# RWKV-7 recurrence of a two-layer decoder step: inverse norms as a power on GpSimd, and another place for the key operations

## What is computed

```python
heads = lambda z: z.reshape(b, t, h, n)               # 16 heads of 64
kk = heads(k * k_k)
kk = kk / jnp.maximum(jnp.linalg.norm(kk, axis=-1, keepdims=True), 1e-12)
k = k * (1 + (a - 1) * k_a)
decay = jnp.exp(-jnp.exp(heads(w)))
# per token: S = S*d - (S kk) (kk*a)^T + v k^T ;  y = S r
mean = jnp.mean(y, axis=-1, keepdims=True)
var = jnp.mean(jnp.square(y - mean), axis=-1, keepdims=True)
y = ((y - mean) * lax.rsqrt(var + RW_GN_EPS)).reshape(b, t, d) * lnx_g + lnx_b
```

## Time and profile before

| what | value |
|---|---|
| median of 3 runs | 3940.99 us (3935.37 to 3941.91) |
| the profiled execution's own time | 3936.94 us |
| its span, first to last instruction | 3935.2 us |
| busy: PE, DVE, ACT, POOL | 93%, 58%, 21%, 19% |
| recurrence, 407 to 1066 us: busy PE, DVE, ACT, POOL | 560.75, 471.37, 252.55, 40.73 us of 659 |
| one pair in the middle, 599 to 675.8 us: the same | 67.32, 59.19, 32.25, 5.22 us of 76.8 |

### The profile page before, as it was taken

One profiled execution on the slowest core, in us unless ns is written; L12 is line 12 of the kernel. 1 busy time (PEld: TensorE's weight loads), 2 busy tenths in 40 slices (PEclk: granted clock), 3 DMA queues, 4 the chain that ended last, 5 costly groups with the idle time before them and its releaser, 6 DMA issues. The chain is left out here.

```text
span 3935.2 us, 73104 instructions
## 1 busy us (share of the span) xinstructions
PE 3673.9 (93%) x31536; PEld 2834.7 (72%) x31536; DVE 2272.5 (58%) x3422; ACT 820.7 (21%) x1836; POOL 742.0 (19%) x504
## 2 busy tenths in 40 slices
PE   7999788888899999999999999999967999999997
PEld 4888566666667888878776777777644788887886
DVE  8442677777456566672646455656546655567253
ACT  6110344433121110110111222222223100101000
POOL 1221000000022222213431100101002222221343
PEclk9999899999999999999999999999989999999999
DMA  2222111011211111122221111111482111112232
GB/s 82 74 81 90 56 36 45 29 36 29 106 39 47 45 45 35 44 75 89 101 79 66 58 40 47 40 47 40 151 307 103 47 45 45 45 43 74 81 113 73
DMA packets 119159, 268.30 MB, mean 68 GB/s; under 512 B 38072, under 2 KB 59960, under 8 KB 116408
## 3 DMA queue, kind: packets, MB, share of 16 engines
q1 hardware_dynamic: 118840, 263.63, 19.4%
HBM read 214.64 MB, written 48.95 MB: 67 GB/s over the span
## 5 line engine op out<-in xcount | busy, mean ns | idle before, releaser
L403 PE MATMUL ps<-sb_h,sb_w 128*128 128x272 f32 x1672 | 408.1, 392 | 1.4 <-ACT sb_tmp L563 1.4
L403 PEld LDWEIGHTS ps<-sb_h,sb_w 128*128 128x128 f32 x1672 | 317.5, 190 | 67.6 <-issue 2.3
L403 PE MATMUL ps<-sb_x,sb_w 128*128 128x272 f32 x1216 | 291.1, 392 | 0.0
L403 PEld LDWEIGHTS ps<-sb_x,sb_w 128*128 128x128 f32 x1216 | 231.0, 190 | 47.6
L460 PE MATMUL ps<-sb_big,sb_w 128*128 128x272 f32 x1056 | 250.9, 396 | 2.5 <-issue 1.3
L460 PEld LDWEIGHTS ps<-sb_big,sb_w 128*128 128x128 f32 x1056 | 202.3, 192 | 46.4 <-issue 4.3
L766 DVE SCALAR_TENSOR_TENSOR sb_big<-sb_tmp,sb_big 128x1024 f32<-128x1024 f32 (+1 forms) x176 | 203.4, 1155 | 13.2
L1454 PE MATMUL ps<-sb_x,sb_w 128*128 128x272 f32 x768 | 183.8, 392 | 0.0
L373 PE MATMUL ps<-sb_h,sb_w 128*128 128x384 f32 (+1 forms) x576 | 177.1, 469 | 3.9 <-DVE sb_tmp L741 2.1
L2693 PE MATMUL ps<-sb_h,sb_w 128*128 128x384 f32 (+1 forms) x528 | 171.8, 468 | 0.0
L1454 PEld LDWEIGHTS ps<-sb_x,sb_w 128*128 128x128 f32 x768 | 145.9, 190 | 30.1
(11 more groups left out here) (413 smaller groups left out, 6972.1 us busy)
## 6 DMA issues: line engine op xcount, KB each, us to landing
sb_w<-wup SPq DMA_DIRECT2D x88, 512.0 KB, 4.5
sb_w<-wdown SPq DMA_DIRECT2D x48, 704.0 KB, 4.2
sb_w<-wqkv SPq DMA_DIRECT2D x33, 512.0 KB, 3.6
sb_w<-wrkv SPq DMA_DIRECT2D x24, 512.0 KB, 5.5
sb_tmp<-wdown SPq DMA_DIRECT2D x16, 704.0 KB, 4.1
sb_x<-kT SPq DMA_DIRECT2D x10, 1024.0 KB, 12.2
rkv_scratch<-sb_big SPq DMA_DIRECT2D x18, 544.0 KB, 6.5
sb_big<-vc SPq DMA_DIRECT2D x9, 1024.0 KB, 11.7
```

The costliest lines, as they stand in the source:

```text
L403: mm = pe.matmul(m.ps[:, 2 * HOME[f][p] + e, 0:PIECE], w, rhs[:, k, e * PIECE:(e + 1) * PIECE], start=(k == 0 and p not in ("P2", "P3")), ...
```

## The change

The root on ACT and the reciprocal on DVE of both norms go. For the key norm DVE takes the sums out of PSUM with a maximum (`square_sums`, behind `t0`) and POOL raises them to the power -0.5; for the norm of y ACT writes scaled sums plus epsilon (`variances`) and POOL raises those. The exponent is a column of -0.5 read again and again. PE waits for POOL, by a new semaphore. `keys` moves from ahead of level 1 to behind level 2. ACT's program holds 26 table loads instead of 39: those of L1723 and L1758 are gone, and one comes in front of the first root of `tail` (L513), whose table the recurrence used to leave behind.

```diff
-    ACTS = numbered([(0, "squares"), (0, "roots"), (0, "powers"), (0, "inverses")],
-                    [(1, "squares"), (0, "queries"), (1, "roots"), (1, "powers"), (1, "inverses"), (-1, "deviations"),
-                     (-1, "deviation_roots"), (0, "U")], [(LAST, "deviations"), (LAST, "deviation_roots")])
+    ACTS = numbered([(0, "squares"), (0, "powers"), (0, "inverses")],
+                    [(1, "squares"), (0, "queries"), (1, "powers"), (1, "inverses"), (-1, "deviations"),
+                     (-1, "variances"), (0, "U")], [(LAST, "deviations"), (LAST, "variances")])
+    NORMS = numbered([(0, "key")], [(1, "key"), (-1, "y")], [(LAST, "y")])
...
         @block.gpsimd
         def _(pool):
             pool.memset(qm, 0.0).then_inc(zeroed, 1)
+            power = m.small[:, 22:23].broadcast_to([P, LANE])
+            pool.memset(m.small[:, 22:23], -0.5)
+            pool.drain()
+
+            def key_norm(j):
+                pool.wait_ge(prep_d, prepared(j, "sums"))
+                pool.tensor_tensor(rootk, rootk, power, ALU.pow).then_inc(normed_by, 1)
+
+            def y_norm(i):
+                pool.wait_ge(acts, ACTS[i, "variances"])
+                pool.tensor_tensor(rootv, rootv, power, ALU.pow).then_inc(normed_by, 1)
+
+            key_norm(0)
             pool.wait_ge(consts, 8 * 16)
             for i in range(PAIRS):
                 for half, (c0, c1) in enumerate(((0, 8), (8, NCH))):
                     wait_taken(pool, i, "at", half)
                     pool.tensor_tensor(AMc[:, c0:c1, :], ATc[:, c0:c1, :], bc(lm[:, 0, :], c1 - c0), ALU.mult).then_inc(am, 1)
+                if i < LAST:
+                    key_norm(i + 1)
+                if i:
+                    y_norm(i - 1)
                 pool.wait_ge(acts, ACTS[i, "U"])
...
+            y_norm(LAST)
...
-            def roots(j):
+            def powers(j):
                 act.wait_ge(small_ps, SUMS[j, "keys"])
-                act.activation(rootk, m.ps[:, 6, 0:LANE], ACT.Sqrt).then_inc(acts, 1)
-
-            def powers(j):
                 act.wait_ge(prep_d, prepared(j, "diff"))
                 act.activation(EP, LS, ACT.Exp, scale=-DEC).then_inc(acts, 1)
...
-            def deviation_roots(i):
+            def variances(i):
                 act.wait_ge(small_ps, SUMS[i, "vars"])
-                act.activation(rootv, m.ps[:, 6, 0:LANE], ACT.Sqrt, bias=m.eps[:, 1:2], scale=1.0 / HD).then_inc(acts, 1)
+                act.activation(rootv, m.ps[:, 6, 0:LANE], ACT.Identity, bias=m.eps[:, 1:2], scale=1.0 / HD).then_inc(acts, 1)
...
-                if ahead:
-                    roots(ahead)
                 turned_out(i, "z0", Yc)
                 if ahead:
                     powers(ahead)
...
-            def inverse_norms(j):
-                dve.wait_ge(acts, ACTS[j, "roots"])
-                dve.tensor_scalar(rootk, rootk, 1e-12, None, ALU.max)
-                dve.drain()
-                dve.reciprocal(rootk, rootk).then_inc(prep_d, 1)
+            def square_sums(j):
+                dve.wait_ge(small_ps, SUMS[j, "keys"])
+                dve.tensor_scalar(rootk, m.ps[:, 6, 0:LANE], 1e-24, None, ALU.max).then_inc(prep_d, 1)
...
-            def inverse_deviations(i):
-                dve.wait_ge(acts, ACTS[i, "deviation_roots"])
-                dve.reciprocal(rootv, rootv).then_inc(gn_d, 1)
...
-            inverse_norms(0)
+            square_sums(0)
...
                 from_one(i, "t0", Xc)
                 if ahead:
-                    keys(ahead)
+                    square_sums(ahead)
                 for l in range(1, 6):
                     level(i, l)
                     if l == 1 and i:
                         center(i - 1)
                     if l == 2 and ahead:
-                        inverse_norms(ahead)
-                    if l == 4 and i:
-                        inverse_deviations(i - 1)
+                        keys(ahead)
                     if l < 5:
                         update(i, f"x{l}", Xc)
...
             def key_norms(j):
-                pe.wait_ge(prep_d, prepared(j, "inv"))
+                pe.wait_ge(normed_by, NORMS[j, "key"])
                 spread(j, "kn", rootk)
...
                 if i + 2 < PAIRS:
-                    pe.wait_ge(acts, ACTS[i + 2, "roots"])
+                    pe.wait_ge(prep_d, prepared(i + 2, "sums"))
...
             def var_norms(i):
-                pe.wait_ge(gn_d, i + 1)
+                pe.wait_ge(normed_by, NORMS[i, "y"])
                 spread(i, "vn", rootv)
```

More of the change, by code:

```diff
@@ L1530, in rwkv_core @@
         full, outd, outa, am = (sem(n) for n in ("psum_full", "dve_out", "act_out", "level_mask"))
-        prep_d, gn_d, acts, small_ps = (sem(n) for n in ("prep_dve", "norm_dve", "act_done", "small_psum"))
+        prep_d, acts, small_ps, normed_by = (sem(n) for n in ("prep_dve", "act_done", "small_psum", "norms"))
         sampw, stp, std, sst, masked, done = (sem(n) for n in ("sample_w", "state_psum", "state", "sample_state", "batch_masked", "pair_done"))
@@ L1572, in rwkv_core @@
         heads = (slice(0, 64), slice(64, 128))
-        EVENTS = ("q0", "diff", "inv", "rkr", "ready")
+        EVENTS = ("q0", "diff", "sums", "rkr", "ready")
         FLAT = ((0, 2 * 384), (2 * 384, T))
@@ L1578, in prepared @@
             if i == 0:
-                return ("q0", "diff", "inv", "keyed", "rkr", "ready").index(event) + 1
+                return ("q0", "diff", "sums", "keyed", "rkr", "ready").index(event) + 1
             return 5 * i + EVENTS.index(event) + 2
@@ L1763, in _ @@
             squares(0)
-            roots(0)
             powers(0)
@@ L1790, in _ @@
                 if i:
-                    deviation_roots(i - 1)
+                    variances(i - 1)
                 turned_out(i, "z3", Yc, PC)
@@ L1806, in _ @@
             deviations(LAST)
-            deviation_roots(LAST)
+            variances(LAST)
         @block.vector
@@ L2059, in _ @@
             center(LAST)
-            inverse_deviations(LAST)
             normed(LAST)
@@ L2308, in _ @@
                 if i:
-                    pe.wait_ge(acts, ACTS[i - 1, "deviation_roots"])
+                    pe.wait_ge(acts, ACTS[i - 1, "variances"])
                 else:
-                    pe.wait_ge(acts, ACTS[1, "roots"])
+                    pe.wait_ge(prep_d, prepared(1, "sums"))
                 pe.wait_ge(ld_s, 16 * (i + 1))
```

## The result

| | before | changed |
|---|---|---|
| median of 4 runs each | 3938.55 us | 4458.4 us (4450.22 to 4464.87) |
| ratio | | 1.1307, 95% interval 1.1291 to 1.1323 |
| span of the profiled execution | 3935.2 us | 4460.4 us |
| mean granted clock of PE | 0.982 | 0.922 |
| recurrence, DVE's first row to PE's first L348 | 658.8 us | 1174.4 us |

The forecast was 3935.9 us, with 3972 as the end of its range. The change costs 520 us between the medians and 525.2 between the two profiled executions; of these 525.2 the recurrence holds 515.6.

What follows compares the result with a forecast made beforehand. No engine is full in the recurrence; PE and DVE wait for each other, DVE late at level 1. 8.4 + 1.3 + 0.8 gained plus 3.8 - 2P at the ends gave 3935.9 us at P = 4.6, range 3927 to 3972.

Steps and rivals of the forecast that it cites:

- The power on POOL: Time P of one power for a norm on POOL: taken as 4.6 us, upper end 13.9.
- Where P shows: Hidden in the middle of a pair up to P = 8.5 us; uncovered at the recurrence's start and end.
- P - 1.7 us lost: Start of the recurrence, where nothing covers the power: 2.9 us lost with P = 4.6.
- P - 2.1: End of the recurrence, PE's spread waiting for the power: 2.5 us lost with P = 4.6.
- 14.3 - 2P: Whole sum: 10.5 us gained in the pairs plus 3.8 - 2P for both ends; 5.1 us less at P = 4.6.
- level 1: Keys moved away, so DVE takes `t1` sooner and PE's wait goes: 1.2 us a pair, 8.4 us for seven.
- level 2: Keys take the place of maximum and reciprocal there: 0.18 us a pair gained, 1.3 us for seven.
- level 4: The y norm's reciprocal on DVE goes, nearly hidden before: 0.12 us a pair, 0.8 us for seven.
- a cheap power: Rival: P near POOL's plain product, 11.5 us gained, 3929.5 us; chance 0.34.
- A dear power: Rival: P above 8.5, PE waits at the y spread in seven pairs and both ends; 3958 us at 9.3; chance 0.22.
- The port held throughout: Rival: a shared port holds DVE's key operations to the end of POOL's power; 4028 us at P = 13.9; chance 0.03.
- Gain taken back: Rival: PE's 1.18 us wait reappears at `x1` or the means, level 1 yields nothing; 3944.3 us; chance 0.06.

Runs made afterwards that it cites:

- Experiment 1: The changed kernel with both powers on POOL replaced by a plain product with a constant, norms not computed: 3932.48 us, ratio 0.9974.
- experiment 6: The kernel before with keys behind level 2 and POOL's power for the key norm only, y by root and reciprocal: 4086.65 us.
- experiment 2: The kernel before with keys behind level 2, the key norm's maximum and reciprocal behind level 3, no POOL work: 3933.16 us, ratio 0.9978.
- experiment 3: The kernel before with both norms on ACT as exponential of a logarithm, keys behind level 2: 3932.57 us, ratio 0.998; repeated 3932.45 us.
- experiment 7: The kernel of experiment 3 with the keys behind level 3 instead of level 2: 3926.69 us, ratio 0.995; repeated 3923.99 us, ratio 0.9954.

## Why the prediction was wrong

**The power on POOL** is the step that failed: the term P of the sum, "0.75 x 6.2 = 4.6 us, which I take", and its bound, "13.9, the upper end". Measured 43.70, 58 times the 0.75 us product it was scaled from (68 times the 0.639 us product in its own place). The scale came from DVE's reciprocal on this tile, another function on another engine, and nothing in the trace of before tied the two; the bound from above rested on how many such steps a power might be made of, which is no measurement either. The Trainium skill's page GPSIMD Engine Reference, section "Side-by-side cycle accounting", with its some 12 cycles for an element in the dearest case, had given an estimated 2.7 us. By the 1.2 GHz that it states, the measured 0.159 us a column is an estimated 191 cycles: the measurement decides, and the page's figure does not cover this operation.

**Where P shows** was right in form, wrong in one sentence. "P - 1.7 us lost" at the start: 42.0 by the formula, and PE's wait there grew by 47.65 - 5.65 = 42.0. "P - 2.1" at the end: 41.6 by the formula, 41.59 measured. But the key norm was called "the less urgent" of the two. POOL takes its list in order: the long key power holds the power for y back, and the wait at the y spread is 62 to 63 us where it is 34 to 36 alone. The prediction's formula, 14.3 - 2P and less P - 8.5 in each of seven pairs, with P = 43.7 gives -73.1 - 7 x 35.2 = -319.5, 4260 us. Missing from it are 178 us of waits, six at the y spread of 62 to 63 us where 35.2 stood and 13.8 us at the key spread of pair 0 for which no term stood, and 22 us that fit the slow clock: 519.5 in all. Experiment 1 gained 14.6 beside the shorter wait at the start, 4.1 more than the 10.5 forecast, which come off; 9.6 come on from outside the recurrence: 525, for 525.2 between the two profiled executions. That the 519.5 also lie by the 519.9 between the medians is chance. That the key's norm has some 30 us of cover (43.7 less the 13.3 of experiment 6) and not more was to be read from the trace of before, and was not: in pair 4 DVE was free for its sums at 751.2, and PE spread the key norm at 784.29.

**The gains.** In pair 4 level 1, taken 1.2 of 0 to 1.65, was 1.55; level 2, 0.18, was 0.08; level 4, 0.12, was 0.04. Over pairs 1 to 6 the first update comes 1.8 us sooner and the y spread 1.9, where 1.5 a pair was forecast: level 1 gave more than it was taken for, the rest next to nothing. ACT was rightly counted at nothing. The 0.28 of level 3 in pair 4 is PE's wait without a named cause, 0.51 before and 0.23 in experiment 1; but in pairs 1 to 3 experiment 1 has such a wait and the kernel before has none. The 0.27 at the closing came in experiment 2 as well, where ACT's table loads were all in place. The one load more in the next stage cost nothing that shows: outside the recurrence experiment 1, which has it, takes 3275.2 us for 3276.4 before. The recurrence of experiment 1 is 15.6 us shorter, where the sum with a cheap power had 11.5. Its mean granted clock was 0.979 for 0.973 before, so part of the 4.1 us more may be the execution's and not the change's; one profile of each cannot tell.

**The rivals.** *A dear power* was the right mechanism at a third of its price: P over 8.5, PE waiting at the y spread in seven pairs and at both ends. Its side cost, 1.05 us for the keys' first instruction beside POOL, did not come: 0.79 us. *The port held throughout* is refuted for this operation: L1834 ended at 728.72, and the power beside it ran to 763.24. The Trainium skill (SBUF — State Buffer, section "SBUF: two separate sides") has the shared pair of ports as an exclusive lock for the whole instruction, for DVE operations of certain kinds; by that rule, if L1834 is of such a kind, it should have stood until 763.24. No run shows which kind it is, but the same form takes 1.83 us beside each of six masked copies. *Gain taken back* is refuted by experiments 1 and 2. *A cheap power* is what experiment 1 made of it: 3932.48 where 3929.5 stood.

**The chances.** The dear power and the held port had 0.25 together, and the range ended at 3972 since P was cut at about 11. A row was missing for the one term on which the sign rested, and the term stood 16 times in the kernel. A guess with a factor of three around it was no bound. The turning point was named wrongly too: "wrong in its sign if one power takes over 8.5 us" stands there, but by the sum itself, 14.3 - 2P, the gain is gone at 7.2 us.

Left over: outside the recurrence the changed kernel takes 9.6 us more (3286.0 for 3276.4), nearly all of it behind the recurrence. PE's products start there at the same time as before for 390 us, later and later from then to some 2100 us, and 9.85 us late from then to the end. The code is the same but for the one table load, which experiment 1 has too. The profiled execution of the repetition of experiment 3, which has no power, also takes 3286.0 us outside the recurrence, and that of experiment 1 takes 3275.2. The mean granted clock behind the recurrence is 0.979 to 0.983 in the four and does not go by their times. So the 9.6 us are as large as the scatter between executions; their cause stays open.

## What to carry to other kernels

An arithmetic function that an engine has not run in the trace has no price; between the plain product and a power on this engine there is a factor of 68. Where the sign of a forecast rests on such a term, work out the price at which the sign turns (7.2 us here), and let a large share of the chance lie beyond it. Price every such term with its neighbours in the queue: here two powers stood one behind the other, and the first held up the second. A move and a replacement that come in one change are worth taking apart: the moved keys alone gave 0.2% and, one level later with the norms on ACT, 0.5%.

## What the runs showed of the hardware

- POOL's tensor-by-tensor power in float32: 0.159 us a column and 0.37 us fixed, the same for 16 and 128 partitions, for exponents of minus one half and one, and for every input here (the real sums, and 2.0 in every place). The product in its place, 272 columns: 0.639 us.
- DVE is not slowed by it: a 1088-column product takes 0.79 us beside the power in all seven pairs (0.76 to 0.79 alone), where the same form beside POOL's masked product took 1.83 us in all six. That a POOL instruction runs is thus not enough to slow DVE; what makes the difference is not shown.
- After 63 us without a product, PE's granted clock read 0.50 for about 5 us. Over the ten waits 22 us are left beside the waits themselves, an estimate of 2.2 us for each.
- ACT's logarithm and the exponential right behind it had a table load each in the runs of experiments 3 and 7 (1.28 us, eight times at either line).
